# Order of the first loads and of the gate work in a two-block kernel: the first chunk's four loads, VectorE's and ScalarE's order up to the queries

## What is computed

```
h = rmsnorm(x, pre_mix_g)
aq, ak, av, hq, hf_fwd, hf_bwd, hi, hg = split_columns(h @ w_in, IN_SPLITS)
...
qf = silu(hq)
f  = lb + (1.0 - lb) * sigmoid(z)          # z = hf_fwd and hf_bwd
o  = bidirectional_gated_scan(qf, log f_fwd, log f_bwd, hi)
...
m  = rmsnorm(mem, mem_norm_g)              # memory rows, for a cross attention later
```

## Time and profile before

| | us |
|---|---|
| median of three runs | 897.18 (897.05 to 897.18) |
| the profiled execution: its own time | 897.12 |
| its span, first to last instruction | 895.3 |
| around the span | 1.82 |

### The profile page before, as it was taken

The page is one execution under the profiler, slowest core; times in us unless marked ns, Lnnn a source line. Parts: engine busy times, 40 slices in busy tenths (PEclk is TensorE's granted clock), DMA queues, the critical chain, the costliest instruction groups (busy, mean ns, idle before and its releaser), DMA issues.

```text
span 895.3 us, 13001 instructions
## 1 busy us (share of the span) xinstructions
PE 880.7 (98%) x4962; PEld 745.3 (83%) x4962; DVE 647.2 (72%) x1021; ACT 496.4 (55%) x883; POOL 89.3 (10%) x123
## 2 busy tenths in 40 slices
PE   8989999999999999999999999999999999999997
PEld 5768897889889888888789888798888888888886
DVE  4688986474778678879857847678687774766774
ACT  4875655574568465566644366676565672424341
POOL 0133300010020000000034300011021200000000
PEclk9999999999999999999999999999999999999999
DMA  7936423553555445647417544345266554554531
GB/s 247 357 102 205 147 101 130 179 174 134 170 190 189 142 143 187 234 151 273 165 59 279 190 166 141 91 156 190 95 213 204 170 189 141 187 208 169 189 141 48
DMA packets 96013, 153.29 MB, mean 171 GB/s; under 512 B 2704, under 2 KB 59280, under 8 KB 95696
## 3 DMA queue, kind: packets, MB, share of 16 engines
q1 hardware_dynamic: 94992, 150.68, 49.3%
q10 hardware_dynamic: 848, 1.52, 0.5%
q0 software_dynamic: 112, 0.26, 0.2%
HBM read 151.40 MB, written 1.05 MB: 170 GB/s over the span
## 4 chain that ended last, share of the span: by engine, by line
PE 83%; DVE 8%; ACT 4%; DMA 2%; issue 2%; POOL 0%; ACTq 0%; DVEq 0%; POOLq 0%; SPq 0%
PE ps L591 23%; PE ps L584 19%; PE ps L1115 13%; PE ps L1119 7%; PE ps L648 6%; PE ps L680 4%; DMA sb_ring<-in_w_in 2%; PE ps L755 2%; DVE sb_wlo L2340 2%; ACT sb_whi L1673 1%; PE ps L766 1%; PE ps L719 1%; PE ps L1063 1%; PE ps L967 1%; PE ps L1259 1%
## 5 line engine op out<-in xcount | busy, mean ns | idle before, releaser
L2340 DVE TENSOR_TENSOR sb_wlo<-sb_ring,sb_whi 128x1024 fp32r<-128x1024 f32 (+2 forms) x168 | 201.7, 1211 | 87.4 <-ACT sb_whi L1673 87.1
L1673 ACT ACTIVATE sb_whi<-sb_ring 128x1024 fp32r<-128x1024 f32 (+2 forms) x168 | 172.8, 1045 | 104.3 <-PE ps L648 68.2
L591 PE MATMUL ps<-sb_whi,sb_tb 128*128 128x512 f32 (+2 forms) x520 | 137.7, 387 | 0.0
L591 PEld LDWEIGHTS ps<-sb_whi,sb_tb 128*128 128x128 f32 x520 | 94.1, 188 | 17.1 <-issue 1.0
L591 PE MATMUL ps<-sb_whi,sb_ta 128*128 128x512 f32 (+1 forms) x328 | 86.4, 388 | 3.4 <-ACT sb_whi L1673 3.4
L591 PEld LDWEIGHTS ps<-sb_whi,sb_ta 128*128 128x128 f32 x328 | 59.2, 190 | 16.9 <-ACT sb_whi L1673 4.9
L648 PE MATMUL ps<-sb_wlo,sb_tb 128*128 128x512 f32 (+2 forms) x224 | 66.7, 380 | 0.0
L1558 POOL TENSOR_SCALAR sb_st<-sb_st 128x1 f32<-128x1 f32 x14 | 7.3, 523 | 451.6 <-ACT sb_probs L1969 451.5
L2298 ACT ACTIVATE sb_b<-sb_b 128x512 f32<-128x512 f32 x9 | 5.7, 632 | 79.7 <-DVE sb_b L2781 79.7
L648 PEld LDWEIGHTS ps<-sb_wlo,sb_tb 128*128 128x128 f32 x224 | 41.5, 188 | 7.8
L2781 DVE TENSOR_REDUCE sb_b<-ps 128x256 f32<-128x512 f32 x36 | 23.8, 685 | 28.2 <-PE ps L1119 28.2
(11 more groups left out here) (430 smaller groups left out, 2009.3 us busy)
## 6 DMA issues: line engine op xcount, KB each, us to landing
sb_ring<-in_w_in SPq DMA_DIRECT2D x31, 1024.0 KB, 6.2
sb_ring<-in_w_up SPq DMA_DIRECT2D x18, 1024.0 KB, 5.1
sb_ring<-in_w_down SPq DMA_DIRECT2D x11, 1024.0 KB, 7.2
sb_ring<-in_w_ffn_down SPq DMA_DIRECT2D x11, 1024.0 KB, 7.4
sb_ring<-in_w_ffn_gate SPq DMA_DIRECT2D x9, 1024.0 KB, 5.1
sb_ring<-in_w_ffn_up SPq DMA_DIRECT2D x9, 1024.0 KB, 5.3
sb_ring<-in_w_xkv SPq DMA_DIRECT2D x8, 1024.0 KB, 5.4
sb_ring<-in_w_out SPq DMA_DIRECT2D x4, 1024.0 KB, 5.5
```

The source lines that it names most:

```text
L591: pe.matmul(o, l, r, start=(start and n == 0), stop=False, skip_group_check=True)
L1673: act.activation(piece_pair(m)[0], src, ACT.Copy).then_inc(s("hi_done"), 1)
L2340: dve.tensor_tensor(low, pieces[m][1], high.bitcast(F32), ALU.subtract).then_inc(s("lo_done"), 1)
```

## The change

In the loads: the four parts of FIRST lose their entries in `raw_before`, so that none of them waits; parts 1, 2 and 3 are started by SP, each behind the part of `turned_x` with its number, and ScalarE's queue keeps only the two halves of F0. GpSimd starts its two loads after four high tiles and no longer after eight. On ScalarE the high part of aq1 is made ahead of the queries' SiLU, no longer behind the memory's tiles. On VectorE the low part of hfb0 stands ahead of the mask rows; `forget("fb")` and the low part of hq3 stand ahead of the scaling of the memory rows; and the low part of aq1 stands ahead of the memory's tiles.

```diff
@@ planner of the loads
                 if name == FIRST:
+                    raw_before[name, j] = []
                     raw_sem[name, j], raw_count[name, j] = s(f"first_w{j}"), 16
                     continue
@@ sync
             for q in range(4):
                 part = slice(KT * (q > 0) + 2 * q * S, KT + 2 * (q + 1) * S)
                 sp.dma_start(turned_x[:, part], a["turned_x"][:, part]).then_inc(s(f"turned_x_in{q}"), 16)
-            load_part(FIRST, 2)
-            load_part(FIRST, 3)
+                if q > 0:
+                    load_part(FIRST, q)
             load_part("hfb", 0)
@@ gpsimd
-            pool.wait_ge(s("first_hi"), KT)
+            pool.wait_ge(s("first_hi"), KT // 2)
@@ scalar
-            dst, w = chunks[0][1][1][1][0]
-            act.dma_start(dst, w.rearrange("(k p) n -> p k n", p=P)).then_inc(raw_sem[FIRST, 1], 16)
...
                 spread_keys(1, "fb")
                 ahead_of("hq", 5)
                 gather_keys(1)
+                ahead_of("hq", 6)
                 for r in range(R):
                     apply("hq", r, hq_rows, ACT.Silu)
...
             pre_norm("mem_norm_g", mem, [[(s("mem_in"), 16)]] * R, memT, gain_at("mem_norm_g"), before_mem)
-            ahead_of("hq", 6)
@@ vector
+            ahead_of("hfb", 1)
             dve.wait_ge(s("const_in"), 16)
...
             ahead_of("hfb", 7)
+            forget("fb", 1)
+            ahead_of("hq", 4)

             def forget_hfb():
-                forget("fb", 1)
                 ahead_of("hq", 5)
                 dve.wait_ge(s("k_ready"), 4)
                 dve.tensor_tensor(kdiag, KD[:, 0:NS], KD[:, NS:2 * NS], ALU.add).then_inc(s("kdiag"), 1)
+                ahead_of("hq", 6)
```

## The result

| | before | after |
|---|---|---|
| median us | 897.18 (897.05 to 897.20) | 890.95 (890.66 to 891.12) |
| profiled execution / its span | 897.12 / 895.3 | 891.1 / 889.3 |

What follows compares the result with a forecast made beforehand. TensorE, busy 98% of the span, was taken to lose mainly in the opening, behind one queued wait, and from backward gate to first level: 5.1 + 1.1 + 1.0 = 7.2 us off 897.18 gives 890.0, range 888.8 to 892.6.

Steps and rivals of the forecast that it cites:

- The opening: F0 to hfb: with F3 no longer queued behind a wait, hfb begins at 17.74, 5.27 us earlier; 5.1 counted.
- rival (b): Loads come at the skill page's 358 GB/s, so a longer stall in hfb; 5.8 in all, 891.4; chance 0.05.
- The stall in hfb: TensorE waits for hfb1's low part near 21.5: a new stall of 0.8 us, 0 to 1.0 by the landings.
- Now VectorE has the mask rows and angles: VectorE after hfb0's low part at 18.0: 3.11 us of mask rows and angles, then hfb1's low part at 22.3.
- No gain or cost of its own: GpSimd's earlier start: positions at 14.5, 3 us before VectorE asks, row vectors and roots moving with them; 0 us.
- The gate region: Backward gate's first half turned to queries turned: 12.1 us for 13.2, hq3's wait of 1.21 gone; gain 1.1.
- aq1: Queries' turning to the scan's first level: 0.78 us of wait gone plus 0.2 counted of the rest; gain 1.0.
- VectorE gets there no later: Up to the first level: VectorE's table work directly follows the memory's tiles, 1.2 us sooner than TensorE needs.
- the prediction's own signs of being wrong: First-level start moves by 7 but the end by less, F3 lands after 14, or VectorE waits for positions.
- Rival (a): New orders only move the waits: the queue gives 5.1, another gate-region wait replaces the old; 892.1; chance 0.13.
- (c): Opening loads: F3 comes no earlier because the engines are full of what stands ahead; 897.2; chance 0.04.
- (d): Slower: GpSimd's positions starve in a full queue, holding VectorE, then TensorE; landing 19 us after issue gives 899; chance 0.04.

Runs made afterwards that it cites:

- without the one line: Changed kernel with VectorE's low part of hfb0 put back behind the mask rows and angles; 895.40 us, ratio 0.9982.
- the joined version: Changed kernel plus hfb1's low part before mask rows, hfb2's high part and sine table before the angles' sine, rotary-table products before memory's tiles; 889.20 us.
- the loads alone: Changed kernel with the earlier gate orders put back and hfb0's low part behind the mask rows, only the load changes kept; 897.63 us, ratio 1.0001.
- the tables moved: Changed kernel with VectorE's eight rotary-table products moved from behind the memory's tiles to ahead of them; 890.52 us, ratio 0.9925.
- the constants' loads first: Changed kernel with ScalarE starting the loads of identity with columns and of tables right behind the halves of F0; 890.93 us, ratio 0.993.

## Why the prediction held, and where it was off

**The opening: right, 5.2.** The reasoning by the queue held at each point that it named: F3 started at about 4 us, hfb begun at 17.84 (17.74 forecast), the positions landed at 8.83 + 5.7 = 14.5 as worked out and nobody waited for them, the clock was 1.00 up to 30 us. hfb's first half landed by 15.65 (15.8). The rate was 371 to 412 GB/s, so rival (b) did not occur. (The full slices of the earlier trace rows run from 19.5 to 39 us, 19.5 us and not the "over 20" of the prediction; nothing hangs on it.)

**But the queue does not own this gain.** My sum put the 5.1 down to the loads and the low part of hfb0 to a subordinate clause. The runs show that neither brings it alone: with the loads and the old orders the forward gate is turned at 34.82, with the line and the gate orders but the old loads at 35.60, where it was 34.54 before; the whole change without the one line wins 1.85, less than the gate orders' 2.7. They are two waits in series: whichever goes alone uncovers the other. The line with nothing else was not run.

**The stall in hfb: the term that was mis-sized.** I had 0.8 (0 to 1.0), it was 1.47 of named wait, and the chunk took 30.54 - 17.84 = 12.70 us in place of 11.7. The step that failed was "Now VectorE has the mask rows and angles", which let them begin as soon as hfb0's low part was done, at 18.0. That needs the tables, and hfb0's low part stands behind the columns; I gave no landing time to the side loads one by one, only let their bytes delay hfb. The columns come at 16.83, so that hfb0's low part ends at 17.19 + 1.22 = 18.41, and the tables land at 10.12 + 8.7 = 18.8, behind hfb's first half: 0.4 us of delay by each. From there the working holds: 3.0 for the angles, 1.2 for the low part, 23.05. Starting the tables early only makes hfb's half late in their place (890.93), and holding back the loads behind hfb's half makes x late (891.76). I take it that what counts is all the bytes up to and with both hfb's half and the tables; taking the row vectors out of them does help (0.6), and so does taking the angles out of the way (0.8).

**"No gain or cost of its own" for GpSimd's earlier start: wrong by about half a microsecond.** It put 256 KB ahead of loads that mattered. I had priced only the positions, which land sooner, and not the row vectors that stand behind them in the same queue: their bytes were in hfb's landing time, but not as a cost of this move. The medians differ by 0.5, the forward gate's start by 0.65.

**The gate region: right.** 12.0 us for a forecast of 12.1, the wait of 1.21 for hq3 gone, ScalarE's path the longer one: ahead of turning the queries TensorE waits 0.20 us for the memory's tiles, which ScalarE makes behind the SiLU. aq1 came out at 1.4 in place of 1.0: both parts were ready, and the 0.6 that I had split between handing over and waiting was mostly waiting.

**"VectorE gets there no later": wrong, 0.65.** I compared VectorE's tables with TensorE's first level and found 1.2 us of cover, and did not go on to the query products and low parts behind them. Once TensorE gains 6.65, VectorE's 6.02 is the smaller of the two, and the difference comes out at aq2. It is the first of the prediction's own signs of being wrong, in small: the first level moved by more than the end. Part of VectorE's loss is the table products: from their first to the queries' products it took 51.72 - 50.17 = 1.55 us in place of 57.74 - 56.54 = 1.20, with GpSimd's totals beside them.

In all: 5.17 in the opening, less 1.2 in hfb, is 4.0 at the forward gate; 1.2 in the gate region and 1.4 at aq1 make 6.65; less 0.65, 6.0. Against the sum of 7.2, the forward gate is 1.1 short and aq2 takes 0.65, while the gate region and aq1 give 0.5 more than forecast; so the total is nearer to its forecast than these two shortfalls alone would put it, and that is luck. Rival (a), a new wait in place of the old, is what happened twice in small, though at neither of its places. (c) and (d) did not occur.

**Left open.** Whether the rest of the 0.65 would come back with GpSimd's totals moved was not run, nor the joined version with GpSimd's later start, which by the two results ought to win a little more. Why ScalarE's two small loads land only with the large one that SP started ahead of them is not settled: the runs show when they land, not by what rule the engines serve them.

## What to carry to other kernels

Before crediting a freed queue with its gain, follow the first thing that it brings early through the order list of each engine that must handle it; if anything in that list waits for another load, the two edits are one and are to be priced together. Beside a full load queue the constants here took 6 to 9 us to land in place of 2.5 or 2.7, so give each its own landing time and ask who waits for it in program order. When one engine is sped up, compare the other's next steps until the first point at which they meet, not only the step beside it.

## What the runs showed of the hardware

- The two small loads on ScalarE's queue took 7.1 us (187 KB) and 8.7 us (272 KB) from start to landing in the changed kernel, beside SP's full queue, where they had taken 2.5 and 2.7. With everything behind hfb's half held back it was still 6.2 and 6.3. GpSimd's two were no slower beside the full queue: 1 KB took 5.7 us and 256 KB 6.5, where they had taken 6.3 and 7.9, started at 13.5 and 14.5, just before the engines filled up again.
- Idleness of TensorE and the granted clock: a gap of 1.47 us left it at 1.00, one of 1.81 us was followed by a stretch of 0.69, ones of 4.13 and 4.15 by 0.81 and 0.85 in one traced execution (the loads alone) and 0.67 and 0.65 in another (without the one line). The executions of each of these two kernels differ by 1.4 us among themselves, with a mean granted clock of 0.994 to 0.998 and of 0.995 to 0.996, so this is not shown to be a difference of the kernels. What a gap costs in clock is not one number, and I would price it by both levels.
- VectorE and GpSimd lengthen each other. GpSimd's totals took 9.56 us in the changed kernel and 14.93 with the tables moved. The longest of them, over 512 elements, took 2.02, 4.22 and 5.31 us in the kernel before, the changed one and that with the tables moved:

```profile
L1583 POOL TENSOR_TENSOR sb_b<-sb_b x12: 215/349/2019, 43.9 to 52.8; 128x512 f32<-128x512 f32 x2, 128x256 f32<-128x256 f32 x2, 128x128 f32<-128x128 f32 x2, 128x64 f32<-128x64 f32 x2
...
L1584 POOL TENSOR_TENSOR sb_b<-sb_b x12: 215/349/4224, 42.2 to 51.6; 128x512 f32<-128x512 f32 x2, 128x256 f32<-128x256 f32 x2, 128x128 f32<-128x128 f32 x2, 128x64 f32<-128x64 f32 x2
...
L1584 POOL TENSOR_TENSOR sb_b<-sb_b x10: 218/830/5311, 42.1 to 53.6; 128x512 f32<-128x512 f32 x2, 128x256 f32<-128x256 f32 x2, 128x128 f32<-128x128 f32 x2, 128x64 f32<-128x64 f32 x2
```

(Rows of the one tile's instructions: durations least/median/most in ns; the third has the ten that began by 54 us.) In the last two the first total ends at 46.43 and 47.43, 0.9 us after VectorE's row of two-operand instructions ends (45.54 and 46.53), as if it had been let in only then; in the kernel before, beside `forget`, the first total took 1.04 us. There one sees it in both directions. The second long total starts at 47.93 beside a low part of VectorE (47.82 to 49.05) and ends at 49.95, 0.9 us after it; VectorE's sum of keys, started at 48.97, takes 2.06 us in place of 1.22 and ends at 51.03, 1.1 us after that total. The lengths are not tied to the order of the tables alone: with F1 on ScalarE's queue, and with the constants' loads first, VectorE's and GpSimd's orders here are those of the changed kernel, but the totals are still running when the query products begin, and take 12.96 us, the products 2.54. The Trainium skill, "SBUF — State Buffer", section Who interferes with whom, states that a VectorE instruction with two SBUF inputs and a GpSimd instruction that reads SBUF exclude each other, the later one waiting until the first is done. These rows agree with it, for a whole row of VectorE instructions too; that VectorE's own instructions grow (2.36 to 3.02) agrees as well. No run here took the totals away to show it by itself.
